# Two transformer-like layers on one core: first transposes among the modulation units, router inside the output product, latent tiles mixed first

## What is computed

```python
sh1, sc1, g1, sh2, sc2, g2 = split(silu(c) @ w_ada + b_ada, 6)
h = rms_norm(x, norm1_g) * (1 + sc1) + sh1
...                                    # three mixers of h @ w_in, gated
x = x + g1 * ((g0*o_mla@w_a + g1_*o_conv@w_b + g2_*o_diff@w_c) @ w_out)
h2 = rms_norm(x, norm2_g) * (1 + sc2) + sh2
# top group of 4, top 2 of its 8 experts, weights from the two softmaxes
x = x + g2 * sum_over_chosen(w_e * (silu(h2@w_gate[e]) * (h2@w_up[e])) @ w_down[e])
# after both layers: rms_norm(x_latent, final_g)
```

## Time and profile before

| | |
|---|---|
| runs | 1679.47, 1675.47, 1680.81 us; median 1679.47 |
| profiled execution | 1675.16 us, its span 1673.3 us |
| TensorE | 1481.9 us busy, 89%, mean granted clock 0.952 |
| weight loads of TensorE | 806.9 us, 48% |
| VectorE, ScalarE, GpSimd | 619.1 (37%), 405.3 (24%), 180.6 (11%) us |
| DMA | 356.49 MB, mean 213 GB/s |
| chain that ended last | TensorE 72%, DMA 14%, VectorE 6%, SyncE's queue 4%, ScalarE 3% |

### The profile page before, as it was taken

The page is one execution under the profiler, slowest core; times in us unless marked ns, Lnnn a source line. Parts: engine busy times, 40 slices in busy tenths (PEclk is TensorE's granted clock), DMA queues, the critical chain, the costliest instruction groups (busy, mean ns, idle before and its releaser), DMA issues.

```text
span 1673.3 us, 18467 instructions
## 1 busy us (share of the span) xinstructions
PE 1481.9 (89%) x7248; PEld 806.9 (48%) x7248; DVE 619.1 (37%) x1389; ACT 405.3 (24%) x914; POOL 180.6 (11%) x144
## 2 busy tenths in 40 slices
PE   3999999999999999889987849999989995997782
PEld 1444444444444445545544437645757764443331
DVE  1178953533234303523211146872433313321112
ACT  3111403432223012212211142403522112221111
POOL 0000410000001110012211100240000100121110
PEclk9899999999999999889998979999999996999997
DMA  7352522112222233569999865542132366999982
GB/s 295 131 202 82 201 100 101 51 51 101 101 101 101 99 152 164 207 252 418 417 419 420 341 247 202 201 183 101 51 151 101 151 251 249 395 419 420 420 367 105
DMA packets 49497, 356.49 MB, mean 213 GB/s; under 512 B 9826, under 2 KB 10210, under 8 KB 16768
## 3 DMA queue, kind: packets, MB, share of 16 engines
q1 hardware_dynamic: 40320, 339.51, 50.1%
q0 software_dynamic: 8224, 12.61, 2.1%
q10 hardware_dynamic: 864, 3.15, 0.5%
HBM read 351.29 MB, written 19.14 MB: 221 GB/s over the span
## 4 chain that ended last, share of the span: by engine, by line
PE 72%; DMA 14%; DVE 6%; SPq 4%; ACT 3%; issue 1%; POOLq 0%; DVEq 0%
PE bank L334 68%; DMA arena<-w_up_in 11%; ACT arena L861 3%; SPq L1921 2%; PE bank L590 2%; DVE arena L1202 1%; SPq L1927 1%; DVE arena L1520 1%; DMA h<-arena 1%; PE bank L760 1%; PE bank L392 1%; DMA arena<-y 1%; DMA routing<-rcon_in 1%; PE bank L774 0%; DMA arena<-h,routing 0%
## 5 line engine op out<-in xcount | busy, mean ns | idle before, releaser
L334 PE MATMUL bank<-arena 128*128 128x512 f32 (+9 forms) x5464 | 1268.3, 464 | 74.4 <-DMA arena<-w_up_in 51.2
L334 PEld LDWEIGHTS bank<-arena 128*128 128x128 f32 (+3 forms) x5464 | 633.0, 158 | 593.0 <-issue 394.3
L861 ACT ACTIVATE arena<-bank 128x512 f32<-128x512 f32 (+7 forms) x536 | 239.5, 471 | 1043.1 <-PE bank L334 919.2
L1202 DVE SCALAR_TENSOR_TENSOR arena<-arena,bank 64x256 f32<-64x256 f32 (+3 forms) x121 | 57.7, 477 | 522.1 <-ACT arena L861 316.8
L1202 DVE SCALAR_TENSOR_TENSOR arena<-arena,vec 128x512 f32<-128x512 f32 (+1 forms) x262 | 182.6, 766 | 0.7
L1439 DVE TENSOR_REDUCE am<-bank 128x1 f32<-128x512 f32 (+1 forms) x96 | 55.5, 599 | 169.5 <-PE bank L334 169.5
L1832 POOL DMA_INDIRECT y<-arena,routing x65 | 63.0, 970 | 387.4 <-ACT arena L861 382.4
L1809 POOL TENSOR_TENSOR arena<-arena 128x512 f32<-128x512 f32 (+1 forms) x32 | 31.9, 996 | 582.1 <-DVE arena L1202 582.1
L861 ACT ACTIVATE arena<-bank,am 128x512 f32<-128x512 f32 (+1 forms) x96 | 58.6, 614 | 77.1 <-DVE am L1442 77.1
L392 PE MATMUL bank<-con,arena 128*128 128x128 f32 x112 | 20.1, 340 | 42.0 <-ACT arena L861 42.0
L334 PE MATMUL bank<-arena,silz 128*32 128x512 f32 x384 | 48.4, 627 | 6.0 <-DMA arena<-ada_in 4.4
(11 more groups left out here) (148 smaller groups left out, 697.2 us busy)
## 6 DMA issues: line engine op xcount, KB each, us to landing
arena<-w_gate_in SPq DMA_DIRECT2D x65, 1024.0 KB, 19.9
arena<-w_up_in SPq DMA_DIRECT2D x65, 1024.0 KB, 28.4
arena<-w_down_in SPq DMA_DIRECT2D x65, 1024.0 KB, 27.4
arena<-ada_in SPq DMA_DIRECT2D x24, 2048.0 KB, 7.8
arena<-mg_in SPq DMA_DIRECT2D x12, 2048.0 KB, 8.2
arena<-mo_in SPq DMA_DIRECT2D x6, 2048.0 KB, 10.5
arena<-glu_in SPq DMA_DIRECT2D x4, 2048.0 KB, 11.1
arena<-out_w_in SPq DMA_DIRECT2D x4, 2048.0 KB, 15.0
```

The costliest lines, as they stand in the source:

```text
L334: return nc.tensor.matmul(out, w, rhs, start=start, stop=stop)
L861: return nc.scalar.activation(out, in_, fn, **kw)
L1202: return V.scalar_tensor_tensor(out, in0, sc, in1, op0=op0, op1=op1)
```

## The change

1. Small loads get semaphores of their own (`cvec_loaded`, `ident_loaded`, `vec_loaded`); con is loaded in two parts, its first 160 columns early, the rest with rcon behind the fifth unit; vecs goes behind the first unit. Lambda's sums come after the shift.
2. The four first tiles get four buffers `xs` and are normed together: four squares, one root, one reciprocal. Their transposes alternate with the units.
3. The router's products and the transposes back stand inside the second half of the next tile's output product (`out_part`, `router_part`). `top2` stands behind the first half's evacuation, `h2_store` before the next norm, and `rank_tile(t - 1)` behind the product.
4. Expert 5's weights wait for the first gather (`xg_ready0`).
5. The last block of each layer is loaded in quarters of gate and up, and TensorE waits for each.
6. In layer 1, g2 is spread before the experts; `y_scaled` on VectorE multiplies while it copies y out, in place of ScalarE's `y_out`. `final_g` is loaded during attention.
7. Mixing: tiles 2 and 3 with their norms and shifts first, then 0 and 1. At the end both latent tiles are mixed before the norms. A Sqrt on a spare column comes before both.
8. Eight more semaphores are shared by the two layers (`seen`).

```diff
-            pe.wait_ge(loaded, 16 * 4)
+            pe.wait_ge(ident_loaded, 16)
             pe.wait_ge(consts_set, 2)
-            for t in range(4):
-                turn_x(0, "n1", t, t)
             pe.wait_ge(silc_ready, 1)
-            for n in ada_behind(None):
-                ada_unit(units[n])
-            ada_finish(None)
+            turn_x(0, "n1", 0, 0, xs[:, 0, :])
+            turn_x(0, "n1", 1, 1, xs[:, 1, :])
+            ada_unit(units[0])
+            turn_x(0, "n1", 2, 2, xs[:, 2, :])
+            ada_unit(units[1])
+            ada_turn(0)
+            turn_x(0, "n1", 3, 3, xs[:, 3, :])
+            ada_unit(units[2])
+            ada_turn(1)
+            ada_unit(units[3])
+            ada_turn(2)
+            ada_turn(3)
...
+                out_tile(qt0, 0)
+                out_tile(qt0, 1)
+                for t in range(qt0 + 1, 4):
                     out_tile(t, 0)
+                    turn_x(l, "n2", NX + t - 1 - qt0, t - 1)
+                    logits = begin("d", ("router", l, t - 1))
+                    ps = begin("d", ("out", l, t, 1))
+                    out_part(ps, t, 1, 0, 4)
+                    router_part(logits, t - 1)
+                    end("d", out_part(ps, t, 1, 4, KD))
+                    rank_tile(t - 1 - qt0)
                 turn_x(l, "n2", NX + 3 - qt0, 3)
...
+                if l == 1:
+                    pe.wait_ge(empty["d"], number["d"][("adaT", 1, NADA - 1)])
+                    spread_rows(l, "g2", ada[l], 5 * KD, TOK)
...
                     for k in range(KD):
+                        if last_block and k % 2 == 0 and k:
+                            pe.wait_ge(quarter_ready[k // 2 - 1], 32 * (l + 1))
...
             for t in range(4):
                 act.wait_ge(x_loaded[t], 16)
+                f(xs[:, t, :], x[:, t, :], ACT.Square, accum_out=st[:, t:t + 1]).then_inc(S[0]["sq_ready"], 1)
+            act.wait_ge(S[0]["sq_ready"], 4)
+            f(st[:, 4:8], st[:, 0:4], ACT.Sqrt, scale=1.0 / D, bias=eps).then_inc(S[0]["ms_ready"], 4)
+            act.wait_ge(S[0]["rs_ready"], 4)
...
+                def y_scaled(e):
+                    p = e % 2
+                    dve.wait_ge(s["y_full"], e + 1)
+                    if e >= 2:
+                        dve.wait_ge(s[f"y_stored{p}"], 16 * (e // 2))
+                    V.tensor_tensor(yy[0:64 + C, p, :], PS[6 + p][0:64 + C, :], g2_halves[0:64 + C, :], op=MUL).then_inc(s["y_act"], 1)
...
                     mixed(0, 2, 0)
-                    mixed(0, 3, 1)
-                    row_norm(S[1], 0, 2)
+                    mixed(0, 3, 1, lambda: row_rstd(S[1], 0))
+                    row_half(S[1], 0, 2)
+                    row_norm(S[1], 1, 3)
+                    shifted(1, "n1", 0, 2)
+                    shifted(1, "n1", 0, 3)
                     mixed(0, 0, 2)
-                    shifted(1, "n1", 0, 2)
-                    row_norm(S[1], 1, 3)
                     mixed(0, 1, 3)
-                    shifted(1, "n1", 0, 3)
...
+                def expert_quarters(j, pairs):
+                    for q in range(4):
+                        for to, src in pairs:
+                            sp.dma_start(to[..., 512 * q:512 * q + 512], src[..., 512 * q:512 * q + 512])                                 .then_inc(quarter_ready[q - 1] if q else gu_ready[j], 16)
...
+                sp.wait_ge(s["xg_ready0"], 16)
                 expert_wd(5)
-                sp.wait_ge(full["a"], A[("back", l, 3, 1)])
                 expert_gu(5)
```

More of the change, by code:

```diff
@@ L867, in take, with raw_copy @@
                 return bank_of[key]
+            def raw_copy(n):
+                ps = take(units[n])
+                give(f(ada_tmp(n), ps[:, :], ACT.Copy))
             def ada_raw(key):
                 for n in ada_behind(key):
-                    ps = take(units[n])
-                    give(f(ada_tmp(n), ps[:, :], ACT.Copy))
+                    raw_copy(n)
             def give(ins):
@@ L1116, in _ @@
                         shifted(l, "n2", 1, t - 1)
+                        h2_store(t - 1)
                     act.wait_ge(s["resid"], 2 * (t - qt0) + 2)
                     row_norm(s, 4 + t - qt0, t)
-                    if t > qt0:
-                        h2_store(t - 1)
                 shifted(l, "n2", 1, 3)
                 h2_store(3)
+                if l == 1:
+                    act.wait_ge(s["xn_d"], 4)
+                    for half in range(2):
+                        r = slice(64 * half, 64 * half + 64)
+                        ps = take(("g2", l, 0, half))
+                        give(f(g2_halves[r, :], ps[r, :], ACT.Copy))
                 act.wait_ge(s["gexp_in"], seen(l, "gexp_in", 1))
@@ L1179, in _ @@
                                 extra(j)
-                row_copies(l, "g2", TOK)
+                if l == 0:
+                    row_copies(l, "g2", TOK)
+                f(small[:, 13:14], small[:, 13:14], ACT.Sqrt)
             for q, t in ((6, 2), (7, 3)):
@@ L1538, in _, with logits_in @@
                 iota = rcon_at(f"place{l}")
+                def logits_in(t):
+                    ps = take(("router", l, qt0 + t))
+                    give(V.tensor_tensor(lg[:, t, :], ps[:, 0:NG + NE], vec_at(l, "b_r"), op=ADD))
                 def top2(t):
```

222 lines of the change are left out of this document (132 added, 90 removed).

## The result

The changed kernel takes 1642.2 us (median of 4 runs, 1639.5 to 1644.4), the kernel before 1678.3 beside it (4 runs): ratio 0.9783, 95% interval 0.9768 to 0.9798. That is 36 us saved where 45 were forecast, inside the range of 1624 to 1649.

What follows compares the result with a forecast made beforehand. TensorE, busy 89% of the span, was taken as the bound, with savings only where it stands still or waits for bytes. 18.0 + 4.2 + 3.3 + 4.2 + 7.1 + 8.6 = 45.4 us off 1679.5 gave 1634, range 1624 to 1649.

Steps and rivals of the forecast that it cites:

- Start: Up to the first big product: earlier turns and fourth unit landing at about 30.0 instead of 42.0; 18 us gained.
- Rival A: Slow start: the clock stays at 1.2 GHz over the mixed start, gain 9 instead of 18, 1643 us; chance 0.14.
- Router and gather: End of output products: router inside the product, weights held, so gather starts earlier; 4.2 us in layer 0, 3.3 in layer 1.
- rival D: Gather stays bound by tables and stores as before; 7.5 becomes 3, 1638.5 us; chance 0.10.
- Quarters: Last block of each expert stage: only 0.9 of up passes after the last landing; 2.1 us per layer, 4.2 in all.
- The rival that they don't pay: Rival C: quarters lose by rate or because the down weights bind; 4.2 becomes −2, 1640 us; chance 0.10.
- Change of layers: Between the layers: context tiles mixed behind the latent tiles' shifts, shifts over at 988.3 instead of 995.4; 7.1 us gained.
- Tail: After the last block: shorter y wait, no g2 multiplications or table load, mixing beside the root; 8.6 us gained.
- Rivals B and E: B: weight stream starts with expert 5, 1650, chance 0.06; E: TensorE keeps 1.2 GHz through 130 us behind start, 1764, 0.02.

Runs made afterwards that it cites:

- e2: Changed kernel with router and turns back of a tile behind the output product again, weights still held back; 1641.1 us, ratio 0.9762 to the kernel before.
- e6: Changed kernel with router logits behind the output product and the last-but-one tile's top-2 behind the last shift; 1631.5 us, ratio 0.9720 to the kernel before.
- e4: Changed kernel with the last block's gate and up weights as two whole loads and one wait; 1646.4 us, ratio 0.9799 to the kernel before.
- e8: Changed kernel with one context tile mixed ahead of the two shifts at the change of layers; 1643.9 us, ratio 0.9807 to the kernel before.
- e11: Changed kernel without the one-element square root that preloads the table behind each expert stage; 1641.8 us, ratio 0.9782 to the kernel before.
- e3: Changed kernel with expert 5's weights no longer held back for the first gather; 1646.5 us, ratio 0.9792 to the kernel before.

## Why the prediction was right, and where it was not

**Start, 18.0 forecast, 14.8 in this profile, 14.7 in the mean of eight** (39.6; 12.1 to 16.7). Mechanism as worked out: the first turn at 15.0 (14.2 forecast), the fourth landing at 31.8 (30.0). The rate was right:

```profile
2.00:32.00 30.00, 13.84 (x100) 8.31 (x104) 5.30 (x13) 12.98 (x23) 0.73 (x1) 1.00 1.00 396
```

What failed first is the count of bytes: I let 11.1 MB pass up to this landing, but 396 GB/s up to 31.8 are 11.8 MB. The fourth unit's weights did not follow alone; glu's were issued at 24.05, 3 us behind them, and shared the queue, and the missing 0.7 MB are the 1.8 us. Then the clock: I had both prices for what follows the landing (5.3 and 8.8 us) and leaned to the fast one; measured were 5.5 in one kernel, 7.1 to 8.9 in the other seven of the same code. So the start has no one value, and 18 lay above the best of them (16.7). Rival A, half speed through the whole start, did not come: units 2 and 3 took 1.92 each.

**Router and gather, 4.2 in layer 0 forecast, −0.35 measured (0.5 in most kernels); 3.3 in layer 1, 0.9 measured.** The gathers behaved, with the store under 5 us: 2.0 gained behind the table against 2.2 in layer 0, and 3.2 in layer 1, where the forecast's terms leave 3.5 to 3.9 (2.9 to 3.3 in all, with 2.0 from the router and 2.6 for the spread at the table). The tables did not: 2.0 earlier was forecast in layer 0, 2.3 later came. Four steps of that working failed. The product ends 4.1 later, not 2.8, since the ranks of one tile more (1.3) now lie ahead of it; "the turn comes 4.1 after the product, as before" was right, but nothing now fills these 4.1, and in this profile the turn ran at half speed (0.9; in most kernels it didn't, which is the difference to their 0.5); from the turn's start to the router I gave 1.8 and it took 3.5, the slow turn included (2.6 in layer 1 with a fast one); and the router ran at 3.60 where I gave 2.4. That is 1.3 + 0.9 + 0.8 + 1.2 = 4.2 of the 4.3 missing. e2 and e6 show what was right instead: the router belongs behind the product, where it hides in the norm's wait, and what had to move was the top-2. In layer 1 the g2 spread cost the tables 2.1, for which I had 2.6, so there too what failed is the router's gain: 2.0 forecast, none measured. Both layers together gained 0.6, less than rival D's 3, but not by its way: the store no longer bound the gather.

**Quarters, 4.2 forecast, about 4 measured** (e4: 1.9 and 2.4 in the stages' means; the ratios' difference, 0.9799 to 0.9783, is 2.7 us with intervals that overlap). The rival that they don't pay is out. The 0.4 for a loss of rate was not measured by itself, and its upper bound of 1.2 is not what the two rates beside it give on 2.1 MB (0.7).

**Change of layers, 7.1 forecast, 7.55 measured.** e8 confirms the mechanism.

**Tail, 8.6 forecast, 7.9 measured.** The table load's 1.28 and my 3.0 for the overlap are right as a sum and not singly: once tile 3 is mixed beside tile 2's root the load costs nothing (e11), and the overlap alone is worth the 4.3 (from the first mixing step to the end 6.8 less, of it 2.5 for the multiplications). What is missing is the new wait for the second tile's y, 0.6 here (0.2 to 1.2 in others), and 0.3 of the wait for the first one's.

**The sum.** In the profiled spans 31.1 instead of 45.4: 3.2 at the start, 4.5 and 2.4 at the routers, 0.7 in the tail; in the experts the profile shows 2.4 of 4.2 (their spread, by e4), and 2.1 went in a stage that the change does not touch; 0.45 more at the change of layers brings it back to 31. The medians, over more executions, give 36. The range held because it left room for a slow start and a gather that gains little, not because the router term was right. Rivals B and E did not show: what the held weights gain is in e3, and the big products were at full speed from about 43 us.

## What to carry to other kernels

Before work is moved into a dense stretch, ask what it was covering where it stood: the router had hidden in a wait that stays when it leaves, and the engine that then idles came back at half clock in 3 of 20 cases here. When the chain crosses two engines, move the part that is late for nobody (here a top-2 of 3.9 us, worth 5 us in two layers) rather than the one that is easy to move. And price a change of a few us by the stage that it is in, over several kernels with the same code there: one pair of profiles had quarters gaining nothing, where ten against two show about 2 us a layer.

## What the hardware did that I had not expected

A single dip of TensorE's clock costs the attention stages 1.7 to 3.1 us (a stage with one more dip against the mean of those without), in a different place in each execution. In the changed kernel it lies here:

```profile
484.00:487.00 3.00, 3.00 (x7) 1.63 (x7) 2.23 (x7) 1.02 (x4) 0.00 (x0) 0.50 0.00 0
```

TensorE is busy throughout; 2 us earlier stands a pause of 0.78 and a group of 128x2 products. The profile before has the same pause and group at 495.86 and no dip. Other kernels with the same code dipped at 246, 290, 393, 483, or not at all, and all changed ones at 1120 to 1135 behind such a group (before at 1149); five again at 1200. Which of these pauses brings a dip stays open.

Where TensorE's work begins the granted clock reads 1.00, yet a group of eight transposes takes 1.7 to 1.8 there and 1.07 to 1.09 later, in every changed kernel; in the kernel before, with 2.2 us of pause between the groups, all four took 1.94 to 1.97. Durations, not the clock's column, tell the speed there; why was not tried.
